# Spreading decay rows over 128 partitions: a copy through DRAM or sixteen small matmuls into PSUM

## The reference, cut to what matters

```
g = -exp(a_log) * softplus(a_alpha + dt_bias)        # (tokens, 8 heads)
G = cumsum(g within a chunk)
diff = G[i] - G[j]
decay = where(i >= j, exp(diff), 0)                  # per head and chunk, 128 x 128
a_kk = (k * beta) @ k.T * decay ;  a_qk = q @ k.T * decay
```

## Time and profile before

| | us |
|---|---|
| time, median of 3 runs (lowest to highest) | 3231.74 (3230.31 to 3234.03) |
| the profiled execution's own time | 3230.31 |
| its span in the trace | 3228.5 |
| PE busy over the span | 2768.7 (86%) |
| DVE / ACT / POOL busy | 1813.8 / 866.2 / 1085.3 |

### The profile page before, as it was taken

One profiled execution on the slowest core, in us unless ns is written; L12 is line 12 of the kernel. 1 busy time (PEld: TensorE's weight loads), 2 busy tenths in 40 slices (PEclk: granted clock), 3 DMA queues, 4 the chain that ended last, 5 costly groups with the idle time before them and its releaser, 6 DMA issues.

```text
span 3228.5 us, 31120 instructions
## 1 busy us (share of the span) xinstructions
PE 2768.7 (86%) x11146; PEld 1836.7 (57%) x11146; DVE 1813.8 (56%) x3673; ACT 866.2 (27%) x1477; POOL 1085.3 (34%) x722
## 2 busy tenths in 40 slices
PE   5989899999898998999889889877777777777776
PEld 3866678876677886878768664433333333333322
DVE  2047133301676643147833357788777777777765
ACT  3245332223575135333453321100100010001000
POOL 2310234443000002445324344444444444444432
PEclk8999899999998999999899999999999999999999
DMA  3200123232420001221112269999999999999997
GB/s 119 79 27 1 52 72 97 91 103 80 157 79 27 1 27 53 94 90 53 61 64 97 85 246 386 385 420 422 422 411 421 410 420 407 420 410 422 412 422 327
DMA packets 115531, 675.54 MB, mean 209 GB/s; under 512 B 16264, under 2 KB 17608, under 8 KB 48976
## 3 DMA queue, kind: packets, MB, share of 16 engines
q0 software_dynamic: 73728, 536.90, 40.4%
q1 hardware_dynamic: 31536, 114.83, 10.6%
q10 hardware_dynamic: 10144, 22.19, 2.0%
HBM read 667.52 MB, written 6.36 MB: 209 GB/s over the span
## 4 chain that ended last, share of the span: by engine, by line
PE 32%; issue 27%; DMA 20%; DVE 13%; POOL 5%; ACT 3%; ACTq 0%; PEldq 0%; POOLq 0%; DVEq 0%; PEld 0%
DMA arena<-in_experts,arena 20%; PE ps L1017 6%; PE ps L431 6%; PE ps L432 6%; PE ps L433 6%; DVE arena L2058 5%; POOL ring_r L2091 4%; PE ps L990 3%; DVE arena L2066 1%; PE ps L600 1%; DVE arena L1894 1%; POOL arena L2126 1%; PE ps L572 1%; DVE arena L1893 1%; DVE arena L1876 1%
## 5 line engine op out<-in xcount | busy, mean ns | idle before, releaser
L2091 POOL TENSOR_TENSOR ring_r<-ring,w_hi 128x1024 fp32r<-128x1024 f32 x191 | 470.7, 2465 | 1353.9 <-ACT w_hi L1040 1230.1
L1017 PE MATMUL ps<-arena 128*128 128x512 f32 x1440 | 691.7, 629 | 204.7 <-DVE arena L2066 204.4
L2126 POOL DMA_INDIRECT arena<-in_experts,arena x502 | 562.1, 1120 | 692.6 <-PE ps L1017 471.6
L1017 PEld LDWEIGHTS ps<-arena 128*128 128x128 f32 x1440 | 273.5, 199 | 617.8 <-DVE arena L2066 327.8
L2058 DVE SCALAR_TENSOR_TENSOR arena<-arena,ring 128x1024 f32<-128x1024 f32 x384 | 465.3, 1223 | 182.2 <-DMA arena<-in_experts,arena 180.4
L431 PE MATMUL ps<-n_hi,w_hi 128*128 128x512 f32 (+1 forms) x1264 | 507.9, 402 | 45.8 <-DVE low L1546 20.0
L433 PE MATMUL ps<-n_hi,ring_r 128*128 128x512 f32 (+1 forms) x1264 | 493.4, 390 | 0.0
L432 PE MATMUL ps<-slot_r,w_hi 128*128 128x512 f32 x896 | 355.1, 396 | 0.0
L1517 ACT ACTIVATE hgel<-hdot 128x2 f32<-128x2 f32 x256 | 52.0, 203 | 1124.1 <-DVE arena L2058 1124.1
L1040 ACT ACTIVATE w_hi<-ring 128x1024 fp32r<-128x1024 f32 x175 | 185.0, 1058 | 569.1 <-PE ps L433 560.0
L431 PEld LDWEIGHTS ps<-n_hi,w_hi 128*128 128x128 f32 x1264 | 240.2, 190 | 121.4 <-issue 45.2
(11 more groups left out here) (332 smaller groups left out, 3979.8 us busy)
## 6 DMA issues: line engine op xcount, KB each, us to landing
ring<-in_weights SPq DMA_DIRECT2D x215, 512.0 KB, 3.5
arena<-in_experts,arena POOLq DMA_INDIRECT x502, 13.0
arena<-decay_rows ACTq DMA_DIRECT2D x2, 2048.0 KB, 11.4
arena<-low_rest ACTq DMA_DIRECT2D x2, 2048.0 KB, 11.7
h_all<-in_xT ACTq DMA_DIRECT2D x1, 2112.0 KB, 16.5
h_rest<-h_all ACTq DMA_DIRECT2D x1, 2048.0 KB, 7.5
low_rest<-slot_r ACTq DMA_DIRECT2D x1, 2048.0 KB, 7.4
h_all<-h_rest ACTq DMA_DIRECT2D x1, 2048.0 KB, 8.4
```

The lines of the kernel that those rows point to most:

```text
L1017: last = mm(ps[:, yb + half, :], diag[:, j, :], rows_of[j][:, D + half * 512:D + half * 512 + 512], start=False, stop=False)
L2091: g_.tensor_tensor(ring_r[:, n % RING], ring[:, n % RING], w_hi[:, n % PAIR].bitcast(F32), ALU.subtract).then_inc(w_ready, 1)
L2126: g_.indirect_dma_start(rows, None, experts, bass.IndirectOffsetOnAxis(ap=idxu[:, t, col:col + 1], axis=0)).then_inc(landed, 16)
```

## The change: what it does

The DRAM tensor and its four DMAs are taken out. PE gets a function `spread`: after each of tiles 8 to 15 it multiplies the one-hot rows `sel[0:H, hd, :]` with `rowG`, and after tiles 16 to 23 with `rows`, into PSUM bank 7, one head each. DVE's two operations read bank 7 instead of the SBUF copy. The one bank is handed to and fro: DVE waits for `bc_ready`, and before the next spread PE waits until DVE has signalled `bc_taken`. The counts of the later users of these semaphores move up by 16.

```diff
-        row_copy = nc.dram_tensor("decay_rows", [2, TT, H, P], F32, kind="Internal")
 # PE
+            def spread(src, hd, bc):
+                if bc == 0:
+                    pe.wait_ge(s["glast_taken"], 1)
+                else:
+                    pe.wait_ge(s["bc_taken"], bc)
+                mm(ps[:, 7, :], sel[0:H, hd, :], src[0:H, :], start=True, stop=True).then_inc(s["bc_ready"], 1)
...
                 if n in (6, 10, 14, 18):
                     sum_heads((n - 6) // 4)
+                if 8 <= n < 16:
+                    spread(rowG, n - 8, n - 8)
+                if n >= 16:
+                    spread(rows, n - 16, n - 8)
                 if n in (21, 22):
...
-                    pe.wait_ge(s["bc_taken"], g - 3)
+                    pe.wait_ge(s["bc_taken"], 2 * H + g - 3)
 # ACT
-                    for i, row in enumerate((rowG, rows)):
-                        act.dma_start(row_copy.ap()[i].rearrange("t h i -> h t i"),
-                                      row[0:H, :].rearrange("h (t i) -> h t i", i=P)).then_inc(s["rows_out"], 16)
-                if n == 4:
-                    act.wait_ge(s["rows_out"], 32)
-                    for i, target in enumerate((DEC, blocks(5))):
-                        act.dma_start(target, bass.AP(row_copy, i * H * SEQ, [[0, P], [H * P, TT], [P, H], [1, P]])
-                                      ).then_inc(s["rows_in"], 16)
...
                 if n == 16:
-                    act.wait_ge(s["dec_set"], H)
+                    act.wait_ge(s["bc_taken"], H)
 # DVE
                 if 8 <= n < 16:
-                    dve.wait_ge(s["rows_in"], 32)
+                    dve.wait_ge(s["bc_ready"], hd + 1)
                     for t in range(TT):
-                        last = v.scalar_tensor_tensor(DEC[:, t, hd, :], DEC[:, t, hd, :], rowT[:, t, 96 + hd:97 + hd],
+                        last = v.scalar_tensor_tensor(DEC[:, t, hd, :], ps[:, 7, t * P:(t + 1) * P], rowT[:, t, 96 + hd:97 + hd],
                                                       const("decay_causal"), ALU.add, ALU.min)
-                    last.then_inc(s["dec_set"], 1)
+                    last.then_inc(s["bc_taken"], 1)
                 if n >= 16:
                     dve.wait_ge(s["dec_exp"], TT)
-                    v.tensor_tensor(LT[:, :, hd, :], DEC[:, :, hd, :], LT[:, :, hd, :], ALU.mult)
+                    dve.wait_ge(s["bc_ready"], H + hd + 1)
+                    v.tensor_tensor(LT[:, :, hd, :], DEC[:, :, hd, :], ps[:, 7, :].rearrange("p (t i) -> p t i", i=P), ALU.mult
+                                    ).then_inc(s["bc_taken"], 1)
...
-                dve.wait_ge(s["bc_ready"], hd + 1)
+                dve.wait_ge(s["bc_ready"], 2 * H + hd + 1)
```

More of the change, by code:

```diff
@@ L290, in build @@
         s = {name: sem(name) for name in (
-            "rows_out", "rows_in", "l2_sq", "l2_sum", "l2_rstd", "l2_done", "small_mm", "row_act", "row_dve", "rowT_ready",
-            "rowT_taken", "bc_ready", "bc_taken", "glast_taken", "dec_set", "dec_exp", "kk_ready", "kk_taken",
+            "l2_sq", "l2_sum", "l2_rstd", "l2_done", "small_mm", "row_act", "row_dve", "rowT_ready",
+            "rowT_taken", "bc_ready", "bc_taken", "glast_taken", "dec_exp", "kk_ready", "kk_taken",
             "tr_ready", "tr_taken", "inv_first", "inv_set", "inv_t", "inv_t_taken", "inv_x", "inv_x_taken", "inv_mask",
```

## The result

The changed kernel takes 3264.23 us (median; 3260.37 to 3268.43), the kernel before beside it 3232.89: a ratio of 1.0094, 95% interval 1.0074 to 1.0114, 31 us more. The forecast had the sign and the place, +23 us and 3255, but not the size: 3264 is just above its range. The profiled execution has a span of 3259.8 us.

The account below looks back on a forecast made before the run. From tile 5 on PE bounds the kernel, so added work adds time: 12.9 spreads + 11.5 stalls - 3.4 old holes + 2.4 clock = +23.4 us, predicting 3255 us, range 3248 to 3263.

Parts of the forecast that it names:

- transfer and its issues: Read back of twice 2 MB, stores and ACT's issues: hidden behind PE's projection work, so removal is worth 0.
- 15 spreads: On PE before the end of tile 23: fifteen added fp32 matmuls at 0.86 us each, 12.9 us.
- waits for the bank: PE stalls for DVE's operation after tiles 9, 13, 17 and 21: 2.9, 1.9, 5.2, 1.5 us, together 11.5.
- old holes filled: PE's present waits after tile 18 (2.4 us) and tile 21 (1.0 us) disappear under the stalls: -3.4 us.
- clock: PE's granted clock falls once, after the 5.2 us stall, adding 2.4 us; the three shorter stalls priced at 0.
- DVE reading PSUM: DVE's two operations take the same time from PSUM as from SBUF: 0.
- The rule that I took from the earlier trace: PE's clock fell to 0.50 after the 3.6 us hole but stayed 1.00 after the 2.4 us hole.
- as dense as elsewhere: PE's 72 matmuls in 15 us under the transfer, used against the 4% rival that the change is not slower.
- dearer: Rival: a spread costs 1.24 us, or the clock also falls after the 2.9 us hole; up to 31.5, 3263; 22%.

Follow-up runs that it names:

- The runs with unread spreads: Kernel before plus sixteen spreads nobody reads: 8 rows 3247.47 us, 128 rows 3245.52 us, 8 rows each done twice 3262.54 us.
- the one with the real ones: Changed kernel with DVE's bank 7 operation first in its loop (except loop 16) and spreads multiplying 128 rows instead of 8: 3250.1 us, ratio 1.0053.
- the second trace: Changed kernel traced and timed again with no edit: 3262.76 us, ratio 1.0088.
- the second pair: Kernel before and changed kernel each traced again, no edit: spans 3233.2 and 3259.4 us; changed kernel 3262.76 us, ratio 1.0088.

## Why the prediction was right or wrong

Its steps, against the first trace of the changed kernel (stage +27.6):

| term | forecast | measured |
|---|---|---|
| transfer and its issues | 0 | 0 (done twice: ratio 1.0004) |
| 15 spreads | 12.9 (0.86 each) | 17.9 (1.19 each, alone) |
| waits for the bank | 11.5 | 8.5 |
| old holes filled | -3.4 | -3.4 |
| clock | 2.4 | 4.2 |
| DVE reading PSUM | 0 | 0 (343, 681 ns) |
| sum | 23.4 | 27.2 of 27.6 |

The clock's 4.2 us are the slowed steps: eight of 0.43 in place of 0.23 after tile 13 (1.6), and after tile 17 a spread of 2.00 in place of 1.05, a step of 0.59 in place of 0.34 and seven of 0.43 (2.6).

- **The step that failed is the price of a spread**, the term "12.9 us": 17.9 were measured. I had both prices, 0.86 from L684 and 1.24 from L774, and chose L684 because its neighbours are those of the projection. The distance that decides is another: L684 multiplies 128 rows like its neighbours, L774 and the spread 8. The runs with unread spreads show it (1.19 on 8 rows, 0.83 on 128, 2.05 for two in a row), and the one with the real ones repeats it. Why the change of rows costs 0.4 us no run shows. The row of the same matmul was the nearer one.
- **The waits** were right in place, number and cause. They came out at 2.4, 1.1, 4.4 and 0.7 in place of 2.9, 1.9, 5.2 and 1.5, that is 0.5 to 0.8 shorter, because each dearer spread (0.4, one or two per wait) brings PE to them later: the first error pays part of itself back. Seven spreads lie on the way to the four waits, 7 x 0.38 = 2.7 us. That their cause is the place of DVE's operation in its loop is shown: put first, three of the four vanish, and the fourth when the exponent is split and loop 16 is put first as well (the two were not tried apart). That it is ACT's root which makes the rest of that loop late is read from the timelines, not from a run without the root.
- **The clock** was mis-sized by 1.8 us, in the second trace by more. The rule that I took from the earlier trace rows, no fall after 2.4 us, one after 3.6, held for its upper half: the 3.6 us hole ahead of tile 4 is followed by a fall in all thirteen traces. Its lower half was one draw. The Trainium skill (TensorE: Matmul & The Clock Gate, "What's actually happening") says that the window in which the chip watches TensorE's activity runs free of the program, and that the point at which the clock changes varies with it. That the same hole may therefore be followed by a fall or not is my inference; the repeated traces agree with it: after the same 2.38 us once 1.00 and once a fall, after 1.1 us once a fall and once none.
- **The transfer** was hidden, as argued, even when doubled. But the 72 matmuls in 15 us that I called as dense as elsewhere include some of the sixteen small ones on 4 columns (L675), so that count proved less than I took it for; the 13.20 and 13.22 us for the same work do prove it.
- **Beyond the stage**: the first pair of traces had 3.7 us more, 2.5 of them ahead of tile 5 and 1.2 after the next stage had begun; the second pair had 1.3 ahead of tile 5 and 2.4 less afterwards. The sum had no term for this. The second pair of timings gives 29 us in all (3262.76 against 3233.57), so part of the 31 may be chance.
- **The size of the miss.** The high case, "dearer", is what happened in the stage, but it was itself summed wrongly: it added the high price without taking the 2.7 us off the waits. Put right it is +26.4 us, 3258, with the high price alone, and +28.8, 3260, with a second fall: inside the range. So of the 9 us between 3255 and 3264 the price explains 2 to 3 net, the clock 1.8, and about 5 lie outside the stage or in the spread of the medians. Without those the time would have come out inside the range, with the same wrong step in it.

## What to carry to other kernels

Here a DMA round trip through DRAM that landed in time cost nothing that could be measured; matmuls put on an engine that is busy in every microsecond cost their full length, and a single bank through which they hand over ties that engine to another one's worst loop. Price an operation by the row that has its own shape (rows, columns, type), before the row that has its neighbours. Where a consumer holds a buffer for the engine that sets the pace, put the consumer's operation first in its loop, ahead of anything that waits for a third engine.

## What the runs showed of the hardware that was not expected

- An fp32 matmul of 512 columns on 8 rows among matmuls on 128 rows costs 1.26 us, on 128 rows 0.86, two on 8 rows in a row 2.11: among such neighbours the one on fewer rows is dearer, and padding it with zero rows saves 0.4 us.
- The same hole does not always bring the clock down. Counted over the thirteen traces, for the wait ahead of tile 4 and those from tile 5 up to the meeting: with a wait of PE of 3.6 us or more the granted clock fell to half (1.2 GHz) in 19 of 19 cases, with one of 2.4 to 2.6 us in 5 of 7, with one of 1.0 to 1.1 us in 1 of 6, and with shorter ones in 0 of 5. Where its cost could be read in the stage, a fall cost 1.6 to 3.1 us.
- The granted clock fell to half (1.2 GHz) behind sixteen small matmuls of 4 columns with no idle time of PE, in one of the traces (875 us, with the transfer doubled), and in the others it did not.
- Programs with the same code ahead of the stage reach it between 829.9 and 836.3 us.
